# Values projected at the head of the mixer chain, and 512-column up-projections

## What is computed

```python
for l in range(DEPTH):
    x = x + 0.5 * swiglu(rms_norm(x, ffn1_norm[l]), ffn1_w_gu[l], ffn1_w_down[l])
    x = x + hybrid_mixer(rms_norm(x, mix_norm[l]), cos, sin, l, w_in[l], ...)
    x = x + 0.5 * swiglu(rms_norm(x, ffn2_norm[l]), ffn2_w_gu[l], ffn2_w_down[l])
```

```python
(aq, ak, av, bq, bk, bv, bf, cq, ck, cv,
 dq, dk, dv, diq, dik, diw) = jnp.split(h @ w_in, points, axis=-1)
...
g = jax.nn.sigmoid(h @ w_gate + b_gate).reshape(B, S, N_BRANCH, D)
merged = (g[:, :, 0] * (ya @ w_br_a) + g[:, :, 1] * (yb @ w_br_b)
          + g[:, :, 2] * (yc @ w_br_c) + g[:, :, 3] * (yd @ w_br_d))
```

## Time and profile before

| | us |
|---|---|
| three runs, median | 4355.12 (4354.69 to 4358.24) |
| the profiled execution, own time | 4361.45 |
| its span, first to last instruction | 4359.6 |
| TensorE matmuls busy in the span | 4012.3 (92%) |
| weight loads busy | 3594.1 (82%) |
| VectorE busy | 3176.9 (73%) |
| ScalarE busy | 2088.8 (48%) |
| GpSimd busy | 555.0 (13%) |
| mean granted TensorE clock | 0.955 of full speed |

### The profile page before, as it was taken

The page is one execution under the profiler, slowest core; times in us unless marked ns, Lnnn a source line. Parts: engine busy times, 40 slices in busy tenths (PEclk is TensorE's granted clock), DMA queues, the critical chain, the costliest instruction groups (busy, mean ns, idle before and its releaser), DMA issues. The chain is left out here.

```text
span 4359.6 us, 68760 instructions
## 1 busy us (share of the span) xinstructions
PE 4012.3 (92%) x24324; PEld 3594.1 (82%) x24324; DVE 3176.9 (73%) x7302; ACT 2088.8 (48%) x4105; POOL 555.0 (13%) x433
## 2 busy tenths in 40 slices
PE   7979999999999998889999998798988999988898
PEld 5569999999788886789998777798867989887697
DVE  7778999898788886679766776554666656558665
ACT  5434433676344443355675554444445444435453
POOL 0000034222222210006770000000000000000000
PEclk9989999999999998999999999899988999999899
DMA  6235488889999984668998886445425444443353
GB/s 240 100 143 185 151 318 303 276 283 325 368 358 348 346 322 149 221 198 212 223 245 262 279 279 215 165 158 166 130 69 195 186 162 185 155 122 118 131 198 135
DMA packets 417963, 939.83 MB, mean 216 GB/s; under 512 B 53258, under 2 KB 242938, under 8 KB 404106
## 3 DMA queue, kind: packets, MB, share of 16 engines
q1 hardware_dynamic: 362380, 801.86, 54.7%
q0 software_dynamic: 55296, 134.31, 9.6%
HBM read 842.60 MB, written 93.42 MB: 215 GB/s over the span
## 5 line engine op out<-in xcount | busy, mean ns | idle before, releaser
L173 DVE TENSOR_TENSOR w_low__2<-w_raw__2,w_high__2 128x512 fp32r<-128x512 f32 x544 | 362.0, 688 | 121.5 <-ACT w_high__2 L168 101.6
L168 ACT ACTIVATE w_high<-w_raw 128x512 fp32r<-128x512 f32 x576 | 343.0, 626 | 210.1 <-PE side L163 88.0
L161 PE MATMUL hidden<-hT_high__2,w_high 128*128 128x384 f32 (+1 forms) x1280 | 426.7, 333 | 10.3 <-DVE w_low L173 10.3
L173 DVE TENSOR_TENSOR w_low<-w_raw,w_high 128x512 fp32r<-128x512 f32 x576 | 382.4, 689 | 73.8 <-ACT w_high L168 70.7
L162 PE MATMUL hidden<-hT_low__2,w_high 128*128 128x384 f32 (+1 forms) x1280 | 422.2, 330 | 0.0
L163 PE MATMUL hidden<-hT_high__2,w_low 128*128 128x384 f32 (+1 forms) x1280 | 421.7, 329 | 0.0
L168 ACT ACTIVATE w_high__2<-w_raw__2 128x512 fp32r<-128x512 f32 x544 | 322.3, 624 | 120.6 <-DMA w_raw__2<-in_peer_v 59.5
L161 PE MATMUL hidden__3<-hT_high__4,w_high__2 128*128 128x256 f32 x1152 | 326.9, 284 | 0.9 <-ACT activated__2 L1420 0.9
L163 PE MATMUL hidden__3<-hT_high__4,w_low__2 128*128 128x256 f32 x1152 | 323.2, 281 | 0.0
L162 PE MATMUL hidden__3<-hT_low__4,w_high__2 128*128 128x256 f32 x1152 | 323.1, 281 | 0.0
L161 PEld LDWEIGHTS hidden<-hT_high__2,w_high 128*128 128x128 f32 x1280 | 245.0, 191 | 11.6 <-issue 11.6
(11 more groups left out here) (975 smaller groups left out, 12147.4 us busy)
## 6 DMA issues: line engine op xcount, KB each, us to landing
w_raw<-in_peer_u SPq DMA_DIRECT2D x128, 512.0 KB
w_raw<-in_peer_v SPq DMA_DIRECT2D x128, 512.0 KB
w_raw__2<-in_peer_u SPq DMA_DIRECT2D x128, 512.0 KB
w_raw__2<-in_peer_v SPq DMA_DIRECT2D x128, 512.0 KB
activated_dram<-activated SPq DMA_DIRECT2D x128, 192.0 KB
routing_dram<-routing SPq DMA_DIRECT2D x24, 1024.0 KB
routing_chunk<-routing_dram SPq DMA_DIRECT2D x16, 1536.0 KB
activated_again<-activated_dram SPq DMA_DIRECT2D x128, 192.0 KB
```

What stands on the lines that cost most here:

```text
L161: nc.tensor.matmul(out, lhs[0], rhs[0], start=start, stop=False, skip_group_check=True)
L168: return nc.scalar.activation(high, src, ACT.Copy)
L173: return nc.vector.tensor_tensor(low, src, high.bitcast(F32), ALU.subtract)
```

## The change

It has two parts.

**Pairs in the feed-forward.** `hT_high` and `hT_low` lie beside each other per chunk (`h_parts`), and `paired_products` multiplies the high part of the weights with both in one matmul of 512 columns, the left half of the bank for high x high and the right for high x low; low x high goes to the left half. So a bank holds two sums side by side, and VectorE adds them (`tensor_reduce`, two per block) into a new buffer `whole`, from which silu and the product read.

```diff
+def paired_products(nc, halves, lhs, pair, start, stop):
+    nc.tensor.matmul(halves, lhs[0], pair, start=start, stop=False, skip_group_check=True)
+    return nc.tensor.matmul(halves[:, 0], lhs[1], pair[:, 0], start=False, stop=stop, skip_group_check=True)
...
-        h_high, h_low = [st.sbuf(x, [P, KC, T], F32R) for x in ("hT_high", "hT_low")]
+        h_parts = st.sbuf("hT_parts", [P, KC, 2, T], F32R)
+        h_high, h_low = h_parts[:, :, 0, :], h_parts[:, :, 1, :]
+        whole = st.sbuf("hidden_sums", [P, 2, parts, T])
...
-                        last = three_products(nc, psA[s][part][:, 0:T], (high[:, p, cut], low[:, p, cut]),
-                                              (h_high[:, k, :], h_low[:, k, :]), k == 0, k == KC - 1)
+                        last = paired_products(nc, psA[s][part][:, :].rearrange("p (x t) -> p x t", x=2),
+                                               (high[:, p, cut], low[:, p, cut]), h_parts[:, k], k == 0, k == KC - 1)
...
-                act.wait_ge(used[UP - 1], j + 2)
+                act.wait_ge(added, parts * j + 1)
                 act.wait_ge(weighted, j + 1)
-                nc.scalar.activation(a[:, s, :], psA[s][0][:, 0:T], combine).then_inc(activated, 1)
+                nc.scalar.activation(a[:, s, :], whole[:, s, 0, :], combine).then_inc(activated, 1)
...
                     low_parts(range(UP), j + 1, 1 - s)
+                for part in range(parts):
+                    dve.wait_ge(used[2 * part + 1], j + 2)
+                    nc.vector.tensor_reduce(whole[:, s, part, :], psA[s][part][:, :].rearrange("p (x t) -> p t x", x=2), X,
+                                            ALU.add).then_inc(added, 1)
                 dve.wait_ge(activated, j + 1)
-                nc.vector.tensor_tensor(a[:, s, :], a[:, s, :], psA[s][1][:, 0:T], ALU.mult).then_inc(gated, 1)
+                dve.wait_ge(added, parts * j + parts)
+                nc.vector.tensor_tensor(a[:, s, :], a[:, s, :], whole[:, s, 1, :], ALU.mult).then_inc(gated, 1)
```

```diff
+VAL_WIDTH = 256
...
+    NV = VALS // VAL_WIDTH
+    VB = NV * KC * VAL_WIDTH // G
+    BLOCKS_IN = VB + NB * KC
...
-        HALVES = 2 * NB * KC
-        share = [(0, 1.25), (IDX_AT, 0.25), (TOP_AT, 2.5), (ATT_AT, 0.5)]
+        HALVES = 2 * BLOCKS_IN
+        share = [(0, 1.25), (IDX_AT, 0.25), (TOP_AT, 2.25), (ATT_AT, 0.9)]
...
+            def value_half(n):
+                b, per = n // 2, 512 // VAL_WIDTH
+                g, first_c = n * per // KC, n * per % KC
+                pe.wait_ge(split, n + 1)
+                if first_c == 0 and g >= 2:
+                    pe.wait_ge(group_kept, g - 1)
+                for c in range(first_c, first_c + per):
+                    at = n % 2 * 512 + (c - first_c) * VAL_WIDTH
+                    cut = slice(at, at + VAL_WIDTH)
+                    for t in range(TT):
+                        rows = slice(t * P, (t + 1) * P)
+                        last = three_products(nc, psg[g % 2][:, t * VAL_WIDTH:(t + 1) * VAL_WIDTH],
+                                              (h_high[:, c, rows], h_low[:, c, rows]),
+                                              (high[:, b % RB, cut], low[:, b % RB, cut]), c == 0 and t == 0,
+                                              c == KC - 1)
+                last.then_inc(used, 1)
...
+                    if o == 0:
+                        pe.wait_ge(group_kept, NV)
...
                 for n in halves[k]:
-                    gate_half(n)
+                    if n < 2 * VB:
+                        value_half(n)
+                    else:
+                        gate_half(n)
...
+            def keep_group(g):
+                act.wait_ge(used, group_end[g] + 1)
+                if g < NV:
+                    nc.scalar.activation(vals[:, :, g * VAL_WIDTH:(g + 1) * VAL_WIDTH],
+                                         psg[g % 2][:, :].rearrange("p (t d) -> p t d", t=TT), ACT.Copy) \
+                        .then_inc(group_kept, 1)
+                    return
...
-        project_rows(nc, w["vals"][l], VALS // 4, 4, KC, hT, range(TT), copy_rows(nc, vals), h_parts)
```

More of the change, by code:

```diff
@@ L711, in gated_mlp @@
         used = st.sems_of("piece_used", NP)
-        activated, gated, gated_high, weighted, own, done = (
-            st.sem(x) for x in ("activated", "gated", "gated_high", "weighted", "dve_wrote", "sum_kept"))
+        activated, gated, gated_high, weighted, added, own, done = (
+            st.sem(x) for x in ("activated", "gated", "gated_high", "weighted", "hidden_added", "dve_wrote", "sum_kept"))
         block = st.begin()
@@ L3073, in mixer_chain @@
     RR, RB, AHEAD, GR = 3, 3, 4, 3
+    NV = VALS // VAL_WIDTH
+    VB = NV * KC * VAL_WIDTH // G
+    BLOCKS_IN = VB + NB * KC
+    group_end = [KC * VAL_WIDTH // 512 * (g + 1) - 1 for g in range(NV)] \
+        + [2 * (VB + d) + 1 for d in range(NB * KC)]
     scale = HD ** -0.5
@@ L3135, in mixer_chain @@
          stick_probs, sticks_ready, scores_ready, max_ready, exp_done, probs_ready, probs_turned, probs_kept, out_ready,
-         out_kept, high_ready, split, used, gate_kept, squared, meaned, rooted, diff_scaled) = (st.sem(n) for n in (
+         out_kept, high_ready, split, used, group_kept, squared, meaned, rooted, diff_scaled) = (st.sem(n) for n in (
              "dve_wrote", "vectors_ready", "dots_ready", "lam_exp", "abs_ready", "ln_done", "exp_step", "cum_ready",
@@ L3201, in weights @@
         def weights(b):
-            return w["gate"][l][b // NB, :, b % NB * G:(b % NB + 1) * G]
+            if b < VB:
+                return w["vals"][l][b]
+            d = b - VB
+            return w["gate"][l][d // NB, :, d % NB * G:(d % NB + 1) * G]
         @block.sync
@@ L3211, in _ @@
             sp.dma_start(pick[:, :], consts["sel4"]).then_inc(landed[4], 16)
-            for b in range(1, NB * KC + 6):
-                if b < NB * KC:
+            for b in range(1, BLOCKS_IN + 6):
+                if b < BLOCKS_IN:
                     if b >= RR:
@@ L3216, in _ @@
                     sp.dma_start(raw[:, b % RR, :], weights(b)).then_inc(w_loaded[b % RR], 16)
-                d = b - 6
+                d = b - VB - 6
                 if d >= 0:
-                    sp.wait_ge(gate_kept, d + 1)
+                    sp.wait_ge(group_kept, NV + d + 1)
                     sp.dma_start(gates_dram[d], gate[:, d % GR, :]).then_inc(gate_stored[d % GR], 16)
@@ L3225, in _ @@
         def _(pe):
+            def value_half(n):
[14 more added lines that the diff above has]
+                last.then_inc(used, 1)
             def gate_half(n):
                 b, half = n // 2, n % 2
+                g = NV + b - VB
                 pe.wait_ge(split, n + 1)
-                if half == 0 and b >= 2:
-                    pe.wait_ge(gate_kept, b - 1)
+                if half == 0:
+                    pe.wait_ge(group_kept, g - 1)
                 for c in range(half * KC // 2, (half + 1) * KC // 2):
                     cut = slice(c * P, (c + 1) * P)
-                    last = three_products(nc, psg[b % 2][:, 0:T], (high[:, b % RB, cut], low[:, b % RB, cut]),
+                    last = three_products(nc, psg[g % 2][:, 0:T], (high[:, b % RB, cut], low[:, b % RB, cut]),
                                           (h_high[:, c, :], h_low[:, c, :]), c == 0, c == KC - 1)
@@ L3351, in make_high @@
                 high_part(nc, high[:, b % RB, cut], raw[:, b % RR, cut]).then_inc(high_ready, 1)
-            def keep_gate(b):
-                act.wait_ge(used, 2 * b + 2)
-                if b >= GR:
-                    act.wait_ge(gate_stored[b % GR], 16 * (b // GR))
-                at = b % NB * KC + b // NB
-                nc.scalar.activation(gate[:, b % GR, :], psg[b % 2][:, 0:T], ACT.Identity, bias=gate_b[:, at:at + 1]) \
-                    .then_inc(gate_kept, 1)
+            def keep_group(g):
[5 more added lines that the diff above has]
+                    return
+                d = g - NV
+                if d >= GR:
+                    act.wait_ge(gate_stored[d % GR], 16 * (d // GR))
+                at = d % NB * KC + d // NB
+                nc.scalar.activation(gate[:, d % GR, :], psg[g % 2][:, 0:T], ACT.Identity, bias=gate_b[:, at:at + 1]) \
+                    .then_inc(group_kept, 1)
             def relu(m):
@@ L3438, in _ @@
                         make_high(n + AHEAD)
-                    if n % 2 and n >= 3:
-                        keep_gate(n // 2 - 1)
-            keep_gate(NB * KC - 1)
+                    if n - 2 in group_end:
+                        keep_group(group_end.index(n - 2))
+            keep_group(NV + NB * KC - 1)
         @block.vector
@@ L4014, in lay_out @@
                                                                      "bk", "cq", "ck")], axis=1)) for l in two])
-    a["vals_2"] = np.concatenate([part[n] for n in ("av", "bv", "cv", "dv")], axis=2)
+    vals = np.concatenate([part[n] for n in ("av", "bv", "cv", "dv")], axis=2)
```

(2 more changed lines are left out.)

2 lines of the change are left out of this document (1 added, 1 removed).

## The result

| us | before | after | forecast |
|---|---|---|---|
| median of 4 runs each, same chip | 4356.68 (4354.69 to 4361.39) | 4327.24 (4325.05 to 4333.4) | 4312 |
| ratio to the kernel before | | 0.9934 (95%: 0.9918 to 0.995) | 0.990 |
| profiled execution, own time | 4361.45 | 4325.75 | 4317.9 |

The kernel is faster, by 29.4 us in the medians where 43.6 were forecast; the time lies inside the range. The two profiled executions differ by 35.7. Of that, 2.7 us lie in the first block of the model, which no edit touches: the first feed-forward's first transfer is issued at 2744.0 for 2746.7. From there to the end it is 1580.1 us for 1612.9, 32.8 less, and this is the number that the steps must explain. One run of the changed kernel in the last group of experiments took 7322.89 us at a mean clock of 0.81 where the others have 0.96; it is in no ratio of this text.

The account below looks back on a forecast made before the run. TensorE was taken to bound the feed-forward and attention, VectorE the top-k part. Four feed-forward stages (-15.6) and two mixer layers (-28) gave -43.6, taking the median from 4355.12 to 4311.5 us; range 4292 to 4336.

Parts of the forecast that it names:

- the top-k part: Mixer chain, ticks 25 to 34: 22 halves for 25, VectorE the bound, so -2.1 us per layer.
- its cover holds: Feed-forward block: VectorE's two added sums, 1.38 us, stay hidden behind TensorE with 2.8 us of slack, costing nothing inside.
- The values' stage: Mixer: the separate stage that projects the values is gone, -34.4 us per layer.
- the place from which the cost comes back: Attention part of the mixer chain: 39 halves of projection work for 16, +22.5 us per layer.
- 0.012 less: Feed-forward: two 256-column matmuls become one of 512, saving 0.012 us per pair, 4.2 us per stage of 352 pairs.
- The first rival: Feed-forward: the pairing gives nothing, a 512-column matmul may cost 0.240 us; total 4328; chance 12%.
- +0.3 at the stage's end: End of each feed-forward stage: with the sums, VectorE takes the first down piece later, +0.3 us per stage.
- I take a cover of 15: Attention part: of 37.5 us of added TensorE work, 15 us is hidden, leaving +22.5 per layer.
- (b): Attention part: TensorE's 24 us at half clock rises to full clock, giving back up to 10.3 us.
- (a): Attention part: added halves fill TensorE's waits, of which the five longest hold 9.0 us.
- The rival without any cover: Attention part: nothing is hidden, growth 37.5 us per layer for 22.5; total 4341; chance 13%.
- the one with more: Attention part hides more, growth 18 us, and the pair saves more than 12 ns; total about 4300; chance 10%.

Follow-up runs that it names:

- e12: The changed kernel itself, run again unaltered on the last chip beside other rate tables; ratio 0.9928 (0.9915 to 0.9941) to the kernel before.

## Why the prediction was right or wrong

**Right.** The time lies inside the range, and the mechanism held in its signs and places; three terms had the wrong size, all told below. What bounds each place: TensorE in the feed-forward, VectorE in the top-k part, TensorE in attention. The sum's duration (0.69 from its nearest row, measured 0.683) and that its cover holds. The values' stage (34.4, measured 34.4 and 34.5 from matmul to matmul), the top-k part (2.1, measured 2.0 and 1.9), and the place from which the cost comes back. The rotation part didn't change with its content: layer 1's +2.6 isn't there in e12 (62.8 for 64.0), and goes with 20.5 us of half clock for 17.1.

**Mis-sized: the pair, "0.012 less".** It saves 0.0075 a chunk, 352 x 0.0075 = 2.6 us a stage. The forecast took 0.228 from a stream of 512-column matmuls alone and 0.120 from one of 256 alone. In the alternating stream of the change the long one has 0.236. The grouped order gives back 0.0025 of the lost 0.0045; what holds the rest wasn't tried and stays open. The first rival (the pairing gives nothing) is excluded: stages are shorter by 2.5 to 3.3, and the pairs alone make the kernel faster with an interval that ends at 0.998. The rule of the Trainium skill (TensorE: Matmul & The Clock Gate, Back-to-back issue gap), 2.5 ns per matmul beside its columns, would have given 0.9 us a stage; the trace does not agree, with 7.5 ns saved per pair. The truth was between that rule and the forecast. The total of 4325 that the prediction gave for the rule (its pairing is worth 4 x 0.9 - 1.2 = 2.4 us by its own numbers, not 1 to 2) and the 4328 of the first rival both lie nearer to 4327.24 than my 4311.5. That is luck and proves neither: only the lengths of the stages tell them apart.

**Wrong and small: "+0.3 at the stage's end".** The wait there is 0.24 us in both kernels. The first of the two sums needs only the first half of the block's up matmuls, so it is taken before the end and silu isn't late; my walk had put both sums behind the last up matmul. ScalarE and VectorE at the end of the first stage of the changed kernel, whose last up matmul starts at 2930.98, and the matmul that waits:

```profile
2928.46 0.69 DVE L830 TENSOR_REDUCE hidden_sums<-hidden 128x256 f32<-128x512 f32 x1 [0.47 <-PE hidden L171]
2929.19 0.42 ACT L798 ACTIVATE activated__3<-hidden_sums 128x256 f32<-128x256 f32 x1 [2.83 <-DVE hidden_sums L830]
2931.29 0.69 DVE L830 TENSOR_REDUCE hidden_sums<-hidden 128x256 f32<-128x512 f32 x1 [2.14 <-PE hidden L171]
...
2932.74 0.63 ACT L791 ACTIVATE pieces_high<-down_raw 128x512 fp32r<-128x512 f32 x1 [3.13 <-PE sum L163]
2932.88 0.43 DVE L838 TENSOR_TENSOR gated_low<-activated__3,gated_high 128x256 fp32r<-128x256 f32 x1
2933.40 0.69 DVE L822 TENSOR_TENSOR pieces_low<-down_raw,pieces_high 128x512 fp32r<-128x512 f32 x1
...
2934.24 0.47 PE L161 MATMUL sum<-pieces_high,gated_high 128*128 128x512 f32 x1 [0.24 <-DVE pieces_low L822]
```

The second sum makes the rest some 0.4 us later, but this ends at 2933.31, just before the high part that VectorE waits for anyway (2932.74 + 0.63 = 2933.37). For four stages the error is 1.2 us, to the good.

With both, a stage wins 2.6, four of them 10.4; in the traces it is 11.1, for 15.6 forecast.

**Mis-sized: "I take a cover of 15".** Measured is 37.5 - 24.7 = 12.8 in layer 0 and 11.5 in layer 1. Its two halves came out apart. (b), the clock: half-clock time fell from 23.9 to 3.4 us, and by the prediction's own rates this is worth an estimated 20.5 x (1 - 1.63 / 2.86) = 8.8, near the full 10.3. In layer 1 13.7 us give 5.9. (a), the waits: of 9.7 us only 1.8 went, in layer 1 3.2 of 11.1. The new halves filled 4.3 us of the old waits, but the one on the probabilities grew to 2.6, and five short ones on the gate's bank are new. The remaining 2 us of each layer aren't assigned. They may lie in the price: where the clock hardly changed, a half cost 1.3 to 1.4 us and not 1.63. The forecast of the part, 108 us at a mean clock over 0.90, was met at 110 and 0.98. The rival without any cover (37.5) and the one with more (18) are both excluded by the lengths.

**The base.** The forecast subtracted from a profiled execution 6.3 us above its median and carried the difference over. The change's profiled one lies 1.5 below its median. So of the 15.7 us between 4311.5 and 4327.2, about 8 are in the steps above (4325.75 for 4317.9, with 2.7 us of luck in the untouched block on the other side), and about 8 are that the two executions stand differently to their medians. That isn't a mechanism of the change; a kernel whose runs spread over 20 us needs it in the range, and the range held it.

## What to carry to other kernels

Merging two matmuls saves the fixed part of one, but read that part from a stream with the mixture that the new code will have: here more than a third of it was missing in a stream of alternating widths, and about half of that came back when like stood with like. Work moved from a stage of its own into a chain isn't hidden because the chain's TensorE shows holes: what it costs is near its full price less what the clock gives back. So ask at each amount whether the clock still rises: here the first 9 pieces and the step from 22 to 30 were cheap, and those between and after were not. When a cover is computed, walk the order of each producer (here, each half of the bank) and not of the block as a whole.

## What was unexpected in the hardware

- A 512-column matmul after a 256-column one, each with its own weights, starts 236 ns before the next, against 229 in the down matmuls and 232 to 234 over the stages in groups of four; a 256-column one 117 for 120.
- VectorE's instructions overlap: sums of 0.68 us follow each other at 0.60 when nothing waits. Costed by their durations, four sums more should have made the block 9.4 us; it was 8.45.
- The attention part without halves ran at 1.2 GHz for 64.9 of 74.1 us although TensorE shows 68.34 busy us there; with 9 halves that fell to some 25 us for 2 us of length, stayed there up to 22 halves, and with a half in nearly each tick was 3.4 of 110.
